# Expert stage of a two-layer diffusion backbone: context tokens routed for all experts at once, and the chosen rows found in four column groups

## What is computed

```python
def expert_choice_ffn(h, w_router, wg, wu, wd):
    N, D = h.shape
    cap = EC_FACTOR * N // N_EXPERTS            # 128 latent rows, 16 context rows for each expert
    aff = jax.nn.softmax((h @ w_router).astype(jnp.float32), axis=-1)
    gate, idx = lax.top_k(aff.T, cap)
    xs = h[idx]
    hid = jax.nn.silu(jnp.einsum("ecd,edf->ecf", xs, wg)) * jnp.einsum("ecd,edf->ecf", xs, wu)
    out = jnp.einsum("ecf,efd->ecd", hid, wd) * gate[..., None].astype(h.dtype)
    return jnp.zeros_like(h).at[idx.reshape(-1)].add(out.reshape(-1, D))
```

## Time and profile before

| | us |
|---|---|
| median of 3 runs | 4265.45 (4264.38 to 4270.08) |
| the profiled execution, its own time | 4266.51 |
| span of its trace | 4264.5 |
| TensorE busy | 3938.3 (92%) |
| VectorE busy | 1844.0 (43%) |
| ScalarE busy | 782.5 (18%) |
| expert stage of layer 0, first gate matmul to last transpose | 1318.2 to 2186.8 |
| expert stage of layer 1, the same | 3355.9 to 4224.5 |

### The profile page before, as it was taken

The page is one execution under the profiler, slowest core; times in us unless marked ns, Lnnn a source line. Parts: engine busy times, 40 slices in busy tenths (PEclk is TensorE's granted clock), DMA queues, the critical chain, the costliest instruction groups (busy, mean ns, idle before and its releaser), DMA issues.

```text
span 4264.5 us, 53100 instructions
## 1 busy us (share of the span) xinstructions
PE 3938.3 (92%) x21940; PEld 2935.4 (69%) x21940; DVE 1844.0 (43%) x4800; ACT 782.5 (18%) x1790; POOL 309.1 (7%) x455
## 2 busy tenths in 40 slices
PE   6979999799987999999979999898999699999996
PEld 2435455644446999999965545666654699999996
DVE  5432012665234444444423314777743444444442
ACT  1112000111020111111120003555532111111112
POOL 0000000000010010011010000010101011111101
PEclk8989999999998999999989999999999799999998
DMA  8750101232334777777760111000013387777776
GB/s 309 250 203 21 40 37 73 79 123 97 120 116 152 270 267 266 262 262 270 254 215 20 40 45 35 1 1 1 1 55 120 127 269 262 262 262 261 264 250 220
DMA packets 281314, 659.18 MB, mean 155 GB/s; under 512 B 9432, under 2 KB 9809, under 8 KB 277810
## 3 DMA queue, kind: packets, MB, share of 16 engines
q1 hardware_dynamic: 245202, 517.05, 33.7%
q0 software_dynamic: 35872, 138.74, 10.6%
HBM read 595.05 MB, written 60.70 MB: 154 GB/s over the span
## 4 chain that ended last, share of the span: by engine, by line
PE 84%; DVE 7%; ACT 5%; DMA 2%; issue 2%; POOL 0%; SPq 0%; DVEq 0%; ACTq 0%; POOLq 0%
PE ps L1005 24%; PE ps L754 13%; PE ps L1024 12%; PE ps L926 6%; PE ps L757 6%; PE ps L723 3%; PE ps L861 3%; PE ps L877 3%; ACT hT L1334 2%; PE ps L1068 2%; PE ps L1069 2%; PE ps L972 1%; PE ps L964 1%; ACT hT L1179 1%; DVE gst L1846 1%
## 5 line engine op out<-in xcount | busy, mean ns | idle before, releaser
L1005 PE MATMUL ps<-big,ring 128*128 128x144 f32 x8192 | 1020.4, 287 | 3.5 <-DVE big L1780 3.5
L1005 PEld LDWEIGHTS ps<-big,ring 128*128 128x128 f32 x8192 | 1010.3, 191 | 9.0 <-issue 8.5
L754 PE MATMUL ps<-hT,ring 128*128 128x384 f32 x1728 | 559.6, 487 | 5.5 <-issue 5.5
L1024 PE MATMUL ps<-big,ring 128*128 128x144 f32 x4096 | 518.0, 288 | 0.0
L1024 PEld LDWEIGHTS ps<-big,ring 128*128 128x128 f32 x4096 | 508.5, 191 | 0.8
L754 PEld LDWEIGHTS ps<-hT,ring 128*128 128x128 f32 x1728 | 328.9, 190 | 235.7 <-issue 8.3
L1780 DVE TENSOR_SCALAR big<-ps,amul,modc 128x128 f32<-128x128 f32 (+1 forms) x512 | 136.4, 342 | 378.9 <-PE ps L973 378.9
L1288 ACT ACTIVATE big<-ps 128x144 f32<-128x144 f32 x256 | 74.5, 291 | 1129.6 <-PE ps L1005 1129.6
L1802 DVE TENSOR_TENSOR big<-big,ps 128x144 f32<-128x144 f32 x256 | 77.9, 304 | 425.1 <-ACT big L1288 421.4
L1846 DVE TENSOR_REDUCE gst<-ps 128x1 f32<-128x1152 f32 x144 | 177.6, 1233 | 168.5 <-PE ps L1070 168.2
L926 PE MATMUL ps<-ring,yT 128*128 128x512 f32 x576 | 247.5, 592 | 0.0
(11 more groups left out here) (312 smaller groups left out, 4142.6 us busy)
## 6 DMA issues: line engine op xcount, KB each, us to landing
ring<-in_moe_wg SPq DMA_DIRECT2D x64, 2048.0 KB, 10.7
ring<-in_moe_wu SPq DMA_DIRECT2D x64, 2048.0 KB, 13.3
ring<-in_moe_wd SPq DMA_DIRECT2D x64, 2048.0 KB, 11.1
ring<-in_w_mod SPq DMA_DIRECT2D x24, 2048.0 KB, 11.2
big<-aff_t POOLq DMA_DIRECT2D x32, 576.0 KB, 4.1
ring<-in_w_in_even SPq DMA_DIRECT2D x7, 2048.0 KB, 7.7
big<-x_res POOLq DMA_DIRECT2D x27, 512.0 KB, 8.4
ring<-in_w_in_odd SPq DMA_DIRECT2D x6, 2048.0 KB, 8.9
```

The lines of the kernel that those rows point to most:

```text
L754: i = mm(ps[:, b + g, 0:384], w[:, k, c * P:(c + 1) * P], hTv[:, k, g * 384:(g + 1) * 384], start=k == 0, stop=k == DK - 1)
L1005: last_mm = mm(ps[:, 3 + f % 2, g * CAP:(g + 1) * CAP], w[u - n0][:, k, c * P:(c + 1) * P], xsT[ee][:, k, :], start=k == 0, stop=k == DK - 1)
L1024: last_mm = mm(ps[:, 3 + d % 2, 0:CAP], w[4 + d // 4][:, k, (d % 4) * P:(d % 4 + 1) * P], hid[:, k, :], start=k == 0, stop=k == DK - 1)
```

## The change

The context leaves the per-expert path. Its affinities are broadcast by TensorE (one-hot column of the identity, widened, against `affT`), ranked for 4 experts ahead of the stage and for 12 experts behind expert 0 (`context_ranks`), gathered by one-hot matmuls (`context_in`) into `xc`, from which each expert takes 16 columns with one copy. Its outputs are collected in `oc`, and after the last expert two one-hot matmuls per half add all of them to `X[:, 8, :]` in SBUF. The gather, the scatter, the transposes and the ranks of each expert are now those of the latent rows alone, and the context tile is no longer written to `xd` and loaded back. Expert 0 is ranked against a row that TensorE puts into PSUM, not against one that went over DRAM. `find` swaps its operands: the 2-column pair is stationary, the one-hot moves (128 columns), and tiles t and t + 4 share one of four column groups; ScalarE copies the 128 x 128 result out (`found_out`), and one more matmul against `sel` (`find_columns`) sums the groups and turns them to columns. `find` now stands before f = 6, `find_columns` before f = 7.

```diff
@@ TensorE, experts
+                pe.wait_ge(*at(m + "affT", 2))
+                for h in range(2):
+                    i = mm(ps[:, 5 + h, :], all_rows(0), affT[:, 512 * h:512 * h + 512], start=True, stop=True)
+                i.then_inc(s(m + "cast"), 1)
                 pe.wait_ge(*at(m + "affT", 3))
+                for e in range(NE):
+                    i = mm(ps[:, e // 4, (e % 4) * P:(e % 4 + 1) * P], all_rows(e), affT[:, LAT:NT],
+                           start=True, stop=True)
...
                 def find(b):
-                    wide = lambda t: tg[:, b, t:t + 1, :].to_broadcast([P, 48, 2])
                     for t in range(8):
-                        mm(ps[:, 7, 0:96], onehot[:, t, :], wide(t), start=t == 0, stop=t == 7)
-                    mm(ps[0:CAPC, 7, 96:192], onehot[:, 8, 0:CAPC], wide(8), start=True, stop=True
-                       ).then_inc(s(m + "ix"), 1)
+                        g = t % 4
+                        i = mm(ps[32 * g:32 * g + 2, 7, 0:P], tg[:, b, t, :], onehot[:, t, :],
+                               start=t < 4, stop=t >= 4, tile_position=(0, 32 * g))
+                    i.then_inc(s(m + "fr"), 1)
+
+                def find_columns(e):
+                    pe.wait_ge(*at(m + "frev", e + 1))
+                    mm(ps[:, 2, 0:96], found_rows, sel, start=True, stop=True).then_inc(s(m + "ix"), 1)
+
+                def context_in(g, ks, bk):
+                    e0, n = ctx_groups[g]
+                    w = n * CAPC
+                    for j, k in enumerate(ks):
+                        i = mm(ps[:, bk, j * w:(j + 1) * w], XN[:, 8, k * P:(k + 1) * P],
+                               ohc[:, e0 * CAPC:e0 * CAPC + w], start=True, stop=True)
+                    i.then_inc(s(m + "cx"), 1)
...
@@ TensorE, after the last expert
+                for d in range(DK):
+                    i = tr(ps[:, d // 4, (d % 4) * P:(d % 4 + 1) * P], oc[:, d, P:2 * P], ident[:, :])
...
+                for half in range(2):
+                    pe.wait_ge(*at(m + "c1ev", half + 1))
+                    hs = slice(512 * half, 512 * half + 512)
+                    mm(ps[:, 3 + half, :], gcT[:, 0, :], octr[:, 0, hs], start=True, stop=False)
+                    mm(ps[:, 3 + half, :], gcT[:, 1, :], octr[:, 1, hs], start=False, stop=True).then_inc(s(m + "cm"), 1)
@@ ScalarE, experts
+                def found_out(e):
+                    act.wait_ge(*at(m + "fr", e + 1))
+                    A(found_rows, ps[:, 7, 0:P], ACT.Copy).then_inc(s(m + "frev"), 1)
@@ VectorE, experts
+                def context_ranks(g):
...
+                    ch(tt(cm3, ctxb[:, es, :], to_all(mine, P), ALU.is_gt))
+                    ch(nc.vector.tensor_reduce(cntc[:, 0, es], cm3, AX.X, ALU.add))
+                    ch(tt(cm3, ctxb[:, es, :], to_all(mine, P), ALU.is_equal))
+                    ch(tt(cm3, cm3, per_e(lower, P), ALU.mult))
+                    ch(nc.vector.tensor_reduce(cntc[:, 1, es], cm3, AX.X, ALU.add))
+                    ch(tt(rankc[:, es], cntc[:, 0, es], cntc[:, 1, es], ALU.add))
+                    ch(tt(oh3, per_e(iota[:, 0:CAPC], CAPC), to_all(rankc[:, es], CAPC), ALU.is_equal))
+                    tt(gc[:, cols].rearrange("p (e c) -> p e c", e=n), oh3, to_all(mine, CAPC), ALU.mult
+                       ).then_inc(s(m + "coh"), 1)
...
+                for t in range(8):
+                    rank_tile(bank(5, 2), 0, t)
                 finish_rank(0)
-                dve.wait_ge(*at(m + "ix", 1))
-                found(0, 0)
-                columns_in(0, 0)
+                dve.wait_ge(*at(m + "cbev", 4))
+                context_ranks(0)
+                found(0)
```

More of the change, by code:

```diff
@@ L566, in experts @@
[L566 to L589, removed]
@@ L978, in experts @@
                 find(0)
-                pe.wait_ge(*at(m + "xs0", 32))
-                turn_in(0)
[L982 to L992, removed]
+                pe.wait_ge(*at(m + "cbev", 4))
@@ new lines, in experts @@
+                            context_in(1, (2 * f, 2 * f + 1), 2)
+                    for d in range(8):
+                        ud_ = n0 + 4 + d // 4
+                        if d % 4 == 0:
+                            landed(pe, ud_)
+                        if d == 0:
+                            pe.wait_ge(*at(m + "hid", 8 * e + 7))
+                        if d == 6 and more:
+                            pe.wait_ge(*at(m + f"xs{1 - b}", 16 * ((e + 1) // 2 + 1)))
+                            turn_in(1 - b)
+                        if d >= 2:
+                            pe.wait_ge(*at(m + "dn", 8 * e + d - 1))
+                        for k in range(DK):
+                            if d == 0 and k == DK - 1:
+                                pe.wait_ge(*at(m + "hid", 8 * e + 8))
+                            last_mm = mm(ps[:, 3 + d % 2, 0:CAP], w[4 + d // 4][:, k, (d % 4) * P:(d % 4 + 1) * P],
+                                         hid[:, k, :], start=k == 0, stop=k == DK - 1)
+                        last_mm.then_inc(s(m + "d"), 1)
@@ new lines, in turn_out @@
+                    def turn_out(c):
+                        return tr(ps[:, 5 + c // 4, (c % 4) * P:(c % 4 + 1) * P], outT[:, c, :], ident[:, :])
+                    pe.wait_ge(*at(m + "rows", e))
+                    pe.wait_ge(*at(m + "dn", 8 * e + 7))
+                    for c in range(7):
+                        turn_out(c)
+                    pe.wait_ge(*at(m + "dn", 8 * e + 8))
+                    turn_out(7).then_inc(s(m + "to"), 1)
+                pe.wait_ge(*at(m + "c0ev", 3))
@@ L1300, in project_odd @@
+                for h in range(2):
+                    act.wait_ge(*at(m + "c1", h + 1))
+                    A(octr[:, 1, 512 * h:512 * h + 512], ps[:, h, :], ACT.Copy).then_inc(s(m + "c1ev"), 1)
             def project_odd():
+                act.wait_ge(*at("x8.stored", 16))
                 for j in range(len(odd_jobs)):
@@ L1824, in experts @@
-                each_expert_pair(pair)
+                dve.wait_ge(*at(m + "cbev", 4))
+                context_ranks(0)
+                found(0)
+                dve.wait_ge(*at(f"o{l}.xn_out", 16 * 8))
+                dve.wait_ge(*at(f"o{l}.x_out", 16 * 8))
+                dve.wait_ge(*at(m + "cxev", 1))
+                columns_in(0)
+                for e in range(NE):
+                    more = e + 1 < NE
+                    b = 1 - e % 2
+                    if more:
+                        dve.wait_ge(*at(m + f"bc{b}", 16 * ((e + 1) // 2 + (b == 1))))
+                        column(b, e + 1)
+                    for f in range(8):
+                        if f == 7 and more:
+                            dve.wait_ge(*at(m + "scattered", e))
+                            found(e + 1)
+                        dve.wait_ge(*at(m + "sg", 8 * e + f + 1))
+                        tt(hid[:, f, :], sg[f % 2], ps[:, 3 + f % 2, CAP:2 * CAP], ALU.mult
+                           ).then_inc(s(m + "hid"), 1)
+                        if more:
+                            for t in ((0, 1), (2, 3), (4, 5), (6, 7), (), (), (), ())[f]:
+                                rank_tile(bc[b], b, t)
+                            if f == 4:
+                                finish_rank(e + 1)
+                    if e == 0:
+                        context_ranks(1)
+                    if more:
+                        columns_in(e + 1)
+                    else:
+                        dve.wait_ge(*at(m + "scattered", e))
+                    dve.wait_ge(*at(m + "to", e + 1))
+                    ts(orow[e % 2], bank(5, 2), gate[:, e % 2, 0:1], None, ALU.mult).then_inc(s(m + "rows"), 1)
@@ L1826, in rope @@
+                for half in range(2):
+                    hs = slice(512 * half, 512 * half + 512)
+                    dve.wait_ge(*at(m + "cm", half + 1))
+                    tt(X[:, 8, hs], X[:, 8, hs], ps[:, 3 + half, :], ALU.add).then_inc(s(m + "xctx"), 1)
             def rope():
```

387 lines of the change are left out of this document (215 added, 172 removed).

## The result

| | before | changed |
|---|---|---|
| median, us | 4266.3 (4264.4 to 4270.1, 4 runs) | 4116.3 (4110.3 to 4122.7, 4 runs) |
| span of the trace | 4264.5 | 4114.2 |
| TensorE busy | 3938.3 | 3833.4 |
| expert stage of layer 0 / 1 | 868.5 / 868.5 | 805.6 / 804.8 |

The account below looks back on a forecast made before the run. TensorE's own instructions were taken to bound the expert stages. Savings of 117.4 us in both stages, 21 in the entries and 4.4 in the exits sum to 142.8, from 4265.4 to about 4123 us, range 4106 to 4150.

Parts of the forecast that it names:

- Rival C: Expert stages: weights land too late, each us beyond 17.8 costs 30; mild form 4153, chance 0.05; slower than before 0.02.
- turn_in: Transposes of an expert's gathered rows on TensorE: sixteen in 3.31 us become eight in 0.95, saving 2.36.
- Way back: Transposes back to rows after an expert's down matmuls: 1.75 us become 1.17, saving 0.58, with ScalarE's last evacuation late.
- find: One-hot products for a next expert on TensorE: 2.12 us become 0.94 (0.70 plus 0.24), saving 1.18.
- the upper bound: For the sixteen new one-hot products of an expert: the pace of the full-width form, 0.118 each, 1.9 us.
- the two changes of mode: Tiling mode switches on TensorE added to the new one-hot products, at 0.10 us each.
- rival D: Expert stages even cheaper: one-hot products at 0.46 us and turns without gaps, 4111; chance 0.03.
- Entry: Ahead of each expert stage: first gate matmul of layer 0 10.7 us earlier, 21 us saved for both layers.
- Exit: Behind each stage: one gate operation and one awaited indirect DMA instead of two, the scatter taking 6.0; 4.4 us together.
- Cover on VectorE: Behind expert 0: context ranks for 12 experts and columns hidden under TensorE's 17.8 us, with 4 us left.
- rival B: VectorE operations with widened operands run at half the pace taken: 24 us lost together, 4147; chance 0.09.

Follow-up runs that it names:

- the sorted turns: The kernel before, with turn_in doing its eight latent transposes first and then its eight 16-row ones, not in turn: 4209.9 us against 4261.7, ratio 0.9867.

## Why the prediction was right

*The bound.* TensorE's own instructions made the stage's length, and no other engine stepped in. Shown by the stretches, busy for the whole 805.6 us. The weight loads kept their cover, but not by much. From 1425 to 2100 the changed kernel's loads took

```profile
DMA to landing us min/median/max: 7.7/12.3/15.5
```

with a median of 12.3 us where it had been 9.6, and in layer 1 one took 16.0. The slowest are the later of the two loads of a first half; one is issued at 1591.95 and wanted at 1608.93, so 17.0 us were there (17.8 forecast) and about 1 was left. Rival C didn't come about; its price per us was not tried.

*turn_in.* 0.95 forecast, 0.87 measured, and the reason (alternation) shown by the sorted turns.

*Way back.* 1.17 forecast, 1.08 measured; that ScalarE's evacuation ends last there is shown.

*find.* 0.94 forecast, 0.75 measured in its two places. The extrapolation from 512 to 128 columns (0.46 at the lower bound) was sound, the upper bound is what one group gives. If 0.46 is taken for the sixteen alone, the two changes of mode make 0.1 us and not 0.2; no run shows them by themselves. These three terms make 0.36 us an expert, of which the period shows 0.26 (50.3 forecast, 50.04 measured), as the gate matmuls around the find are slower by the rest. That is why the stages gave 63 us each and not 58.7. With 126.6 for both they lie nearer to rival D (129) than to the forecast (117.4).

*Entry.* 21 forecast, 16.8 measured: the term that was sized too large. Of its steps, the row came 3.8 us after the affinities (3.3 had been taken), the context ranks took 4.2 (4.0), and from the gather's landing to the first gate matmul it was 4.1 us and not 3.2: all eight column operations run behind the first transposes, 2.65 us, where I had counted the last four. (The prediction's own terms end at 1307.3, not at its 1307.5.) Layer 1 was taken to be like layer 0 and wasn't: its entry before was 1.4 us shorter already, and its gather took 5.3 us after and 4.3 before.

*Exit.* In layer 0 the step "one indirect DMA is awaited" stood, but the 6.0 us given to it failed. They held for the kernel before, at this very place too, and were carried over as if a scatter's duration were its own. It depends on how long the weight loads go on behind its issue, and the change moved one against the other: 8.59 us. At the end of the kernel, where no weights follow, it is 6.00 and the forecast holds.

*Cover on VectorE.* Four us were forecast and found; rival B's halved pace is refuted by the trace, where a 1536-column operation takes 1.75 us with widened operands, 2.1 having been taken:

```profile
1339.38 1.75 DVE L1887 TENSOR_TENSOR hT<-yT 128x1536 f32<-128x1536 f32 x1
```

The total was closer than its parts, and part of that is luck: 5 us of the 150 come from untouched code, the stages gave 9 more than forecast and the entries and the exits 7 less.

## What to carry to other kernels

When the timeline shows one engine without gaps, read its small instructions by start-to-start time and compare with the pace of the same form standing together; a pace twice as slow points at the order, and sorting is two lines where rerouting is a rewrite. In this kernel products with few stationary columns got cheap only in several column groups at once. And don't carry the duration of a DMA over from the kernel before when the change moves it against the large loads: ask how long those will go on behind its issue.

## What the runs showed of the hardware

- Alternating 128-row and 16-row transposes costs about 0.12 us each time; sorted, the 16-row ones take 0.07 us each.
- Sixteen float32 instructions with 2-column weights and 128 moving columns take 0.55 us in four column groups, 1.83 in one.
- A wait of 5.93 us of TensorE cost 8.6, as the clock fell to 1.2 GHz for some 4.5 us behind it.
- A scatter of 128 rows takes 6.00 us at the end of the kernel and 6.29 at the exit of layer 0 with weight loads held back. With loads that go on for 3 us behind its issue it took 6.0, with 5 us of them 8.59.
